# A gated-delta and latent-attention encoder step on one core: norm's end and the squares of q one level up, attention's branch first in the out stage

## The reference, cut to what matters

```python
u_a = o_a * silu(z_a)                       # delta branch
u_b = o_b * silu(z_b)                       # attention branch
merged = sigmoid(g_a) * (u_a @ w_o_dn) + sigmoid(g_b) * (u_b @ w_o_mla)
y = x + gate[:, None, :] * (merged @ w_out)
```

```python
vnew = u_ - w_ @ S
o = qg_ @ S + attn_ @ vnew
S = S * gl_[..., None, None] + swapaxes(kd_, -1, -2) @ vnew
```

## Time and profile before

| | us |
|---|---|
| median of 3 runs | 2172.28 |
| lowest to highest | 2171.09 to 2174.40 |
| the profiled execution | 2174.75 |
| its span | 2173.1 |
| PE busy in the span | 1972.0 (91%) |
| DVE, ACT, POOL busy | 886.9, 700.0, 199.6 |
| delta stage, about | 1472 to 1853 of the span |
| out stage, about | 1853 to the end |

### The profile page before, as it was taken

One profiled execution on the slowest core, in us unless ns is written; L12 is line 12 of the kernel. 1 busy time (PEld: TensorE's weight loads), 2 busy tenths in 40 slices (PEclk: granted clock), 3 DMA queues, 4 the chain that ended last, 5 costly groups with the idle time before them and its releaser, 6 DMA issues.

```text
span 2173.1 us, 32025 instructions
## 1 busy us (share of the span) xinstructions
PE 1972.0 (91%) x12297; PEld 1825.1 (84%) x12297; DVE 886.9 (41%) x1840; ACT 700.0 (32%) x1528; POOL 199.6 (9%) x248
## 2 busy tenths in 40 slices
PE   6899999999999999958875789997989988899899
PEld 2799999999999999947764677876989988799877
DVE  1555454010010010046443565556667667424332
ACT  2433333111111122122323454435565664211110
POOL 0022121000000000000002221112010010000000
PEclk9999999999999999979995999998999999899999
DMA  9222222222223222141101221132131213623322
GB/s 318 70 102 93 93 101 105 100 94 112 82 93 112 82 93 99 44 141 39 35 17 57 68 59 45 40 107 74 40 97 60 78 59 108 227 82 107 97 98 72
DMA packets 153724, 195.61 MB, mean 90 GB/s; under 512 B 9153, under 2 KB 124910, under 8 KB 153628
## 3 DMA queue, kind: packets, MB, share of 16 engines
q1 hardware_dynamic: 142300, 151.85, 20.8%
q0 software_dynamic: 10064, 38.13, 5.2%
q10 hardware_dynamic: 1264, 4.39, 0.5%
HBM read 134.15 MB, written 60.19 MB: 89 GB/s over the span
## 4 chain that ended last, share of the span: by engine, by line
PE 77%; DVE 10%; issue 4%; ACT 4%; DMA 2%; DVEq 2%; ACTq 1%; POOLq 1%; POOL 1%; SPq 0%
PE PS L2124 39%; PE PS L1275 9%; PE PS L1436 8%; PE PS L1372 4%; PE PS L1441 3%; PE PS L376 3%; PE PS L713 2%; PE PS L688 2%; PE PS L2140 1%; PE PS L674 1%; PE PS L701 1%; DMA Wraw<-in_w_ada 1%; ACT E L1610 1%; DVE amx L922 1%; PE PS L383 1%
## 5 line engine op out<-in xcount | busy, mean ns | idle before, releaser
L2124 PE MATMUL PS<-HH,WL 128*128 128x352 f32 (+1 forms) x1752 | 380.1, 325 | 5.2 <-DVE mod L2234 5.2
L2124 PE MATMUL PS<-HH,WH 128*128 128x352 f32 (+1 forms) x1752 | 378.4, 323 | 0.0
L2124 PE MATMUL PS<-HL,WH 128*128 128x352 f32 (+1 forms) x1752 | 378.0, 324 | 0.0
L2124 PEld LDWEIGHTS PS<-HH,WL 128*128 128x128 f32 (+1 forms) x1752 | 299.0, 189 | 5.6 <-issue 5.3
L2124 PEld LDWEIGHTS PS<-HH,WH 128*128 128x128 f32 (+1 forms) x1752 | 301.1, 188 | 0.3
L2230 DVE TENSOR_TENSOR WL<-Wraw,WH 128x2048 fp32r<-128x2048 f32 x37 | 84.8, 2293 | 523.0 <-ACT WH L2067 523.0
L2124 PEld LDWEIGHTS PS<-HL,WH 128*128 128x128 f32 (+1 forms) x1752 | 297.8, 188 | 0.2
L2095 ACT ACTIVATE R<-PS 128x1056 f32<-128x1056 f32 x48 | 50.6, 1053 | 409.2 <-PE PS L2124 409.1
L1436 PE MATMUL PS<-WT,QL 128*128 128x128 f32 x832 | 102.2, 276 | 1.7 <-DVE QL L1824 0.9
L1660 ACT ACTIVATE WT<-PS 128x512 f32<-128x512 f32 x104 | 62.1, 597 | 123.1 <-PE PS L1436 123.1
L713 PE MATMUL PS<-V,pT 128*128 128x128 f32 (+1 forms) x624 | 87.2, 284 | 14.4 <-ACT pT L804 14.2
(11 more groups left out here) (290 smaller groups left out, 3196.5 us busy)
## 6 DMA issues: line engine op xcount, KB each, us to landing
scratch_proj<-R SPq DMA_DIRECT2D x72, 576.0 KB, 2.8
Wraw<-in_w_in POOLq DMA_DIRECT2D x36, 1024.0 KB, 5.4
QKV<-scratch_proj SPq DMA_DIRECT2D x27, 512.0 KB, 5.2
Wraw<-in_w_ada SPq DMA_DIRECT2D x12, 1024.0 KB, 6.2
fr<-scratch_u SPq DMA_DIRECT2D x16, 528.0 KB, 5.3
gr<-scratch_proj SPq DMA_DIRECT2D x16, 528.0 KB, 3.6
qraw<-scratch_proj SPq DMA_DIRECT2D x9, 768.0 KB, 5.0
zb<-scratch_proj SPq DMA_DIRECT2D x18, 256.0 KB, 3.2
```

What stands on the lines that cost most here:

```text
L2124: last = pe.matmul(PS[0:m, psum + b, 0:TB], w[:, s, k, c * P:c * P + m], h[:, k, b * TB:(b + 1) * TB], start=(k == 0 and first), stop=(k = ...
```

## The change

It does three things. In the delta stage DVE's `dve_norm_end` stands at the end of level 3, and ACT's squares of q of group 1 stand in level 2, behind those of group 0. In the out stage the attention's branch (rows 8 to 15 of scratch_u, w_o_mla, the gate rows g_b) is computed first. Its first four rows are loaded in the delta stage, behind the two weight loads, into fr, which has another place in memory; and the gate's matmuls, diagonals and copies move from ahead of the first chunk into chunks 3 and 4, with banks 6 and 7 and a tile GD of their own.

```diff
@@ tiles
     p4a = ExitStack()
+    GD = sb(p4a, "GD", [P, 2, D])
+    NFR = 4
+    fr = sb(p4a, "fr", [P, NFR, TOK])
+    VH = sb(p4a, "VH", [P, 2, KD, 256], F32R)
+    VL = sb(p4a, "VL", [P, 2, KD, 256], F32R)
     FH = sb(p4a, "FH", [P, KD, TOK], F32R)
     FL = sb(p4a, "FL", [P, KD, TOK], F32R)
...
-    GD = M4[:, 0:2, 0:D]
@@ sp_out
-        for r in range(KD):
+        for r in range(NFR, KD):
             row(r)
-            if r == 3:
+            if r == NFR:
                 for n in range(2):
                     sp_gate_rows(sp, n)
@@
+    def sp_u_row(sp, r):
+
+        sp.dma_start(fr[:, r % NFR], scr["u"][(r + H) % (2 * H), :, 0:TOK]).then_inc(s_fr[r % NFR], 16)
+
     def sp_w_o(sp, l):
-        w = a["w_o_dn"] if l < 4 else a["w_o_mla"]
+        w = a["w_o_mla"] if l < 4 else a["w_o_dn"]
@@ dve_branches
-        dve_gate(dve)
         split_w(0)
         for r in range(2 * KD):
             if r == KD:
                 split_w(1)
+                dve_gate_diagonal(dve)
                 for n in range(KD - 1):
                     merge(n)
+                    if n == 2:
+                        dve_gate(dve)
@@ pe_branches
         for n in range(2 * KD):
             l = n // 2
+            if n in (3, 4):
+                for i in range(2):
+                    gate_rows(2 * (n - 3) + i)
@@ sp_delta
         for l in range(2):
             sp_w_o(sp, l)
+        for g in range(2):
+            sp.wait_ge(d_qs, nth(NT - 1, g))
+        for r in range(NFR):
+            sp_u_row(sp, r)
         sp_store_u(sp, NT - 2)
@@ act_delta
                 if l == 2 and more:
                     act_decays_of(act, n + 1, "relu")
                     act_q(act, n + 1, 0)
+                    act_q(act, n + 1, 1)
                 if l == 3:
-                    if more:
-                        act_q(act, n + 1, 1)
@@ dve_delta
                     dve_norm_steps(dve)
+                    dve_norm_end(dve, p, w)
                 if l == 4:
-                    dve_norm_end(dve, p, w)
                     if t is not None:
                         dve_state(dve, t, 1)
```

More of the change, by code:

```diff
@@ L1099, in build @@
     p4a = ExitStack()
+    GD = sb(p4a, "GD", [P, 2, D])
[3 more added lines that the diff above has]
+    VL = sb(p4a, "VL", [P, 2, KD, 256], F32R)
     FH = sb(p4a, "FH", [P, KD, TOK], F32R)
     FL = sb(p4a, "FL", [P, KD, TOK], F32R)
[L1102 to L1105, removed]
     gr = sb(p4a, "gr", [P, 2, TOK])
-    sb(p4a, "branches_spacer", [P, 5368])
+    sb(p4a, "branches_spacer", [P, 3320])
     Vraw = sb(p4a, "Vraw", [P, 2, KD, 256])
@@ L1145, in row @@
                 sp.wait_ge(s_fl, r - NFR + 1)
-            sp.dma_start(fr[:, r % NFR], scr["u"][r, :, 0:TOK]).then_inc(s_fr[r % NFR], 16)
+            sp_u_row(sp, r)
         def weights(l):
@@ L1182, in sp_w_out @@
         sp.dma_start(Vraw[:, i % 2], a["w_out"][0, :, 256 * i:256 * i + 256].rearrange("(k p) n -> p k n", p=P)).then_inc(s_vr[i % 2], 16)
+    def sp_u_row(sp, r):
+        sp.dma_start(fr[:, r % NFR], scr["u"][(r + H) % (2 * H), :, 0:TOK]).then_inc(s_fr[r % NFR], 16)
     def sp_w_o(sp, l):
-        w = a["w_o_dn"] if l < 4 else a["w_o_mla"]
+        w = a["w_o_mla"] if l < 4 else a["w_o_dn"]
         sp.dma_start(Vraw[:, l % 2], w[0, :, 256 * (l % 4):256 * (l % 4) + 256].rearrange("(k p) n -> p k n", p=P)).then_inc(s_vr[l % 2], 16)
     def sp_gate_rows(sp, n):
-        sp.dma_start(gr[:, n % 2], scr["proj"][C_GA + n, :, 0:TOK]).then_inc(s_gr[n % 2], 16)
+        sp.dma_start(gr[:, n % 2], scr["proj"][C_GA + (n + KD) % (2 * KD), :, 0:TOK]).then_inc(s_gr[n % 2], 16)
     def act_out(act):
@@ L1212, in act_out, with dve_gate_diagonal @@
             split_w(l)
-    def dve_gate(dve):
+    def dve_gate_diagonal(dve):
         for i in range(4):
@@ L1219, in dve_gate @@
                               mod[:, j:j + 4, s:s + 1].to_broadcast([P, 4, P]), ALU.mult).then_inc(s_gdg, 1)
+    def dve_gate(dve):
         for i in range(4):
             dve.wait_ge(s_gps, i + 1)
-            dve.tensor_copy(gate[:, i // 2, 512 * (i % 2):512 * (i % 2) + 512], PS[:, i]).then_inc(s_gok, 1)
+            dve.tensor_copy(gate[:, i // 2, 512 * (i % 2):512 * (i % 2) + 512], PS[:, 6 + i % 2]).then_inc(s_gok, 1)
     def dve_branches(dve):
@@ L1260, in pe_branches, with gate_rows @@
     def pe_branches(pe):
-        for i in range(4):
+        def gate_rows(i):
             pe.wait_ge(s_gdg, i + 1)
-            pe.matmul(PS[:, i], ones, GD[:, i // 2, 512 * (i % 2):512 * (i % 2) + 512], start=True, stop=True).then_inc(s_gps, 1)
-        pe.wait_ge(s_gok, 4)
+            if i >= 2:
+                pe.wait_ge(s_gok, i - 1)
+            pe.matmul(PS[:, 6 + i % 2], ones, GD[:, i // 2, 512 * (i % 2):512 * (i % 2) + 512], start=True, stop=True).then_inc(s_gps, 1)
         for n in range(2 * KD):
             l = n // 2
+            if n in (3, 4):
+                for i in range(2):
+                    gate_rows(2 * (n - 3) + i)
             pe.wait_ge(s_vl, l + 1)
```

## The result

The changed kernel takes 2137.37 us (median of 4 runs, 2136.05 to 2139.18), against 2172.70 of before (4 runs, 2171.09 to 2174.40). The ratio is 0.9838, with a 95% interval of 0.9821 to 0.9855: 35 us faster, where 36.1 were forecast (2136.2, range 2130 to 2147).

What follows compares the result with a forecast made beforehand. PE was taken to be bound by pauses for the mask-delayed state update. Pauses 22.9, clock 8.3, squares 3.9 and out stage 1.0 make 36.1 us off 2172.28: 2136.2 us, range 2130 to 2147.

Steps and rivals of the forecast that it cites:

- What bounded the step: Delta stage: masks hold norm's end, which holds the state update; PE waits 3.0 us for it in seven steps.
- The price of the pause: Delta stage, products of level 4 to level 5: 8.15 us against 4.88 at full clock, 3.27 in each of seven steps.
- The clock: PE's clock falls behind five of seven pauses at 1.65 us each: 8.3 us gained, bounds 0 to 11.6.
- Norm's end free, update beside the masks at no cost: Delta stage: norm's end fits DVE's idle time in level 3, and the update does not wait for masks; cost 0.
- The cover: Level 3: norm's end, about 1.1 us long, is done 0.6 us before POOL's first mask.
- margin of the update: Level 4: the state update ends 0.75 us before PE comes to the attended product.
- The squares: Group 1's squares of q in level 2 let PE's turns start 0.55 us earlier in seven steps, 3.9 us.
- The out stage: PE starts 5.9 us earlier, chunk 0 ends 4.5 earlier, gate matmuls take back 3.5; net 1.0 us gained.
- Early rows in SP's queue: Four early rows ahead of the last stores take 6.2 us, hidden: cost 0, without cover up to 6.2.
- Step 0: Delta stage's first step, without state update: 0 to 1 us gained, taken as 0.

Runs made afterwards that it cites:

- e4: Kernel before, norm's end still in level 4, but GpSimd waits for it before a tile's first mask; 2143.38 us against 2175.25, ratio 0.9859.
- e5: Changed kernel plus 15 small DVE reductions ahead of the state update of group 1; 2161.69 us against 2174.10 of the kernel before, ratio 0.9945.
- e1: Kernel before with only norm's end moved to the end of level 3; 2142.21 us against 2175.25, ratio 0.9844.
- e2: Kernel before with only group 1's squares of q moved to level 2; 2164.86 us against 2175.25, ratio 0.9955.
- e3: Changed kernel with both delta-stage edits undone, only the out stage changed; 2175.21 us against 2175.25 of the kernel before, ratio 1.0003.
- e12: The kernel of e2 (only the squares moved) timed and profiled once more; 2164.79 us against 2175.17 of the kernel before, ratio 0.9953.
- e7: Changed kernel with the two gate rows loaded behind row 7 instead of row 4; 2136.86 us against 2174.10 of the kernel before, ratio 0.9826.
- e10: Changed kernel with the first two gate matmuls and their diagonals ahead of chunk 0; 2136.52 us, ratio 0.9825 to the kernel before.
- e6: Changed kernel plus 8 small DVE reductions ahead of the state update of group 1; 2144.57 us, ratio 0.9859 to the kernel before.

## Why the prediction was right

**What bounded the step.** Norm's end, held by the masks, held the state update, and that held PE. e4 shows the first link alone, e5 the last alone, and e1 the sum. The price of the pause, 3.27 us, was exact: 4.88 us remain. The Trainium skill ("SBUF — State Buffer", the practical consequences of the shared port pair) has a DVE instruction held by GpSimd when it has two SBUF inputs or runs in a two-port mode. The prediction says that the trace agrees, by the 1.15 us of L1766; this one has a single input tensor, in SBUF, so it agrees only if it ran in such a mode, which no run shows. The sum does not hang on it.

**The clock.** 5 x 1.65 = 8.3 us, and with the pause it is gone. The cost of a fall, 1.65 us, came again in e2, e3, e5 and e12. The five falls are those of one profile: e3, with the same delta stage, had six, and e2 and e12, with nearly the same, three. So this term may be anything from 5 to 10 us, and that the sum came within 1 us of the measured gain is in part luck.

**Norm's end free, update beside the masks at no cost.** The cover was thin as said: 0.76 us ahead of the first mask, forecast 0.6; from the end of L98 the norm's end took 0.88 us, forecast 1.1; margin of the update 0.71 us, forecast 0.75. The copies of level 4, which begin with the mask, took 1.53 us in this step instead of 1.35, and 1.36 to 1.38 in the six others: a small delay, hidden.

**The squares.** 0.55 us a step beside the moved norm's end: 35.83 (e1) to 35.29, right. As a term on its own it was mis-sized: alone the edit gave 10 us, and its profiles show a shorter wait in step 1 and fewer falls of the clock beside the 0.47 us a step. The terms do not add up: e1's 34, e2's 10 and e3's 0 make 44, and the whole is 35 to 39. A fall that the squares alone would save is saved by the norm's end already.

**The out stage.** Chunk 0 ended 4.5 us earlier (T + 21.05 against T + 25.5 before). That this is the forecast figure is chance in part: the prediction took its T + 21.6 from the first merge at T + 26.1, which starts 0.5 us behind the chunk, so from end to end it had 3.9, and the wait for row 5 was 0.4 shorter than its 2. The gate's pair among the chunks costs 1.7 us (1859.11 to 1860.42, and 0.40 in the spacing of the next matmul), 3.4 in all against 3.5. The net gain of 1.0 us is 1.1 in the two profiles; over all of them the stage up to the first output matmul is 208.1 to 208.8 us in the five with the old out stage and 207.7 to 208.2 in the six with the new, 0.4 apart in the mean. It is under what the times tell. The gain of the early rows went where the forecast put it, into the gate's new place and the gate rows in the queue; e7 and e10 get back 2 us from each.

**Early rows in SP's queue.** Hidden: 2.43 us from DVE's last u to the meeting, before 2.42.

**Step 0.** Taken as 0; from its first mask to that of step 1 it takes 33.02 us instead of 33.77, a gain of 0.75 inside the 0 to 1 that were allowed.

The profiled executions differ by 38.7 us, more than the medians. 3.7 of them lie ahead of the delta stage (its first mask is at 1477.07, before 1480.73), in stages that nobody touched; other profiles of these kernels have it at 1477.5 to 1482.7.

## What to carry to other kernels

An instruction of 128x8 elements that shows over 1 us need not be slow; it may be standing still. Here 0.17 us of work took 1.15: look for what ended together with it, here a GpSimd instruction on another tile. What it costs is decided by what stands behind it in its queue and who waits for that, and it is cured as well by moving the small one as by holding back the long one. Price a pause of PE with the clock behind it, and treat edits that shorten the same pause as one term.

## What the runs showed of the hardware that was not expected

The granted clock falls behind some pauses and not behind others of the same length. For the pauses of 2.6 to 3.1 us the counts are five of seven (before), six of seven (e3), three of seven (e5) and three of six (e2 and e12 each). Behind 1.0 us (seven cases in e6) it never fell. And PE work at the lower clock ahead of a gap of under 1 us (e10) did not bring the full clock forward.
